# LayerNorm rows of the last two blocks as bf16 rows in DRAM, read back by 32 transposing DMAs

## What is computed

```
proj = h @ w_in                                  # q, k, v, c_gate, b_gate, u
attn = sliding_window_attention(rope(q), rope(k), v, sinks)     # window 128
conv = b_gate * causal_conv3(c_gate * u)
mixed = concat([rms_norm(attn), rms_norm(conv)])
h = layer_norm(ALPHA * h + mixed @ w_out)        # LayerNorm 1
ffn = (silu(h @ w_gate) * (h @ w_up)) @ w_down
h = layer_norm(ALPHA * h + ffn)                  # LayerNorm 2
```

## Time and profile before

| | us |
|---|---|
| median of 3 runs | 2705.77 |
| the profiled execution, by the same measure | 2704.75 |
| its span, slowest core (core 6) | 2703.7 |
| spans of the eight cores | 2693.0 to 2703.7 |
| first half (four blocks), by the first gate/up matmul | 0 to 864.5 |
| feed-forward half | 864.5 to the end |

### The profile page before, as it was taken

The page is one execution under the profiler, slowest core; times in us unless marked ns, Lnnn a source line. Parts: engine busy times, 40 slices in busy tenths (PEclk is TensorE's granted clock), DMA queues, the critical chain, the costliest instruction groups (busy, mean ns, idle before and its releaser), DMA issues.

```text
span 2703.7 us, 33712 instructions; the slowest of 8 cores (2693.0 to 2703.7 us)
## 1 busy us (share of the span) xinstructions
PE 2641.0 (98%) x13266; PEld 1213.2 (45%) x13266; DVE 716.1 (26%) x1454; ACT 497.8 (18%) x922; POOL 99.5 (4%) x191
## 2 busy tenths in 40 slices
PE   6999999998999999999999999999999999999998
PEld 2444444443444444444444444444444444444443
DVE  1445454553553300111111111124200111111026
ACT  1433433432432200000000001122100000000021
POOL 1010010010000000000000000000000000000000
PEclk9999999999999999999999999999999999999999
DMA  9999999999999795334554435557833354434352
GB/s 161 186 187 182 198 184 192 196 184 182 205 189 205 160 250 89 60 66 77 94 86 71 79 59 132 91 106 206 186 64 65 65 102 78 82 67 80 61 106 109
DMA packets 46619, 347.36 MB, mean 128 GB/s; under 512 B 4864, under 2 KB 4992, under 8 KB 19072
## 3 DMA queue, kind: packets, MB, share of 16 engines
q0 software_dynamic: 26928, 256.39, 56.9%
q1 hardware_dynamic: 19536, 88.82, 9.5%
HBM read 559.62 MB, written 41.94 MB: 222 GB/s over the span
## 4 chain that ended last, share of the span: by engine, by line
PE 93%; DMA 4%; DVE 1%; issue 1%; ACT 0%; POOL 0%; DVEq 0%; ACTq 0%; POOLq 0%
PE ps L316 92%; DMA w<-w_qkv 4%; PE ps L320 1%; DVE rowsf L357 0%; DVE atok L342 0%; ACT pT L336 0%; DVE y L357 0%; DVE small L622 0%; DVE ropeA L342 0%; ACT y L336 0%; DVE small L342 0%; DVE zc L342 0%; DVE ropeB L342 0%; POOL xT L366 0%; DVE h1Ts L360 0%
## 5 line engine op out<-in xcount | busy, mean ns | idle before, releaser
L316 PE MATMUL ps<-h1T,w 128*128 128x512 bf16 x5632 | 1216.9, 379 | 0.0
L316 PEld LDWEIGHTS ps<-h1T,w 128*128 128x128 bf16 x5632 | 550.9, 98 | 663.6
L316 PE MATMUL ps<-w,actT 128*128 128x512 bf16 x2640 | 571.6, 379 | 0.0
L316 PEld LDWEIGHTS ps<-w,actT 128*128 128x128 bf16 x2640 | 258.3, 98 | 311.5
L342 DVE TENSOR_TENSOR actT<-ps,sg 128x512 bf16<-128x512 f32 x176 | 121.8, 692 | 1026.4 <-PE ps L316 1009.2
L336 ACT ACTIVATE sg<-ps 128x512 f32<-128x512 f32 x176 | 105.1, 597 | 1320.4 <-PE ps L316 1315.2
L316 PE MATMUL ps<-xT,w 128*128 128x512 bf16 x1536 | 344.9, 380 | 0.0
L316 PEld LDWEIGHTS ps<-xT,w 128*128 128x128 bf16 x1536 | 147.6, 98 | 181.1 <-issue 14.0
L316 PE MATMUL ps<-w,mT 128*128 128x512 bf16 x1024 | 222.3, 379 | 0.0
L357 DVE SCALAR_TENSOR_TENSOR rowsf<-rowsf,ps 128x512 f32<-128x512 f32 x128 | 88.0, 688 | 468.1 <-PE ps L316 468.1
L316 PE MATMUL ps<-w,xT 128*128 128x512 bf16 x768 | 177.4, 388 | 31.8 <-DMA w<-w_qkv 29.3
(11 more groups left out here) (102 smaller groups left out, 858.1 us busy)
## 6 DMA issues: line engine op xcount, KB each, us to landing
w<-w_gu POOLq DMA_DIRECT2D x44, 2048.0 KB, 16.0
w<-w_cbu POOLq DMA_DIRECT2D x32, 1536.0 KB, 32.8
w<-w_down POOLq DMA_DIRECT2D x30, 1408.0 KB, 12.0
w<-w_out POOLq DMA_DIRECT2D x32, 1024.0 KB, 24.6
w<-w_qkv POOLq DMA_DIRECT2D x18, 1024.0 KB, 43.8
h_scr<-rows SPq DMA_DIRECT2D x16, 1024.0 KB, 22.0
rowsf<-h_scr SPq DMA_DIRECT2D x16, 1024.0 KB, 24.2
xT<-xT_c POOLq DMA_DIRECT2D x16, 512.0 KB, 36.7
```

Source lines behind the costliest of these rows:

```text
L316: pr.add("pe", lambda e: e.matmul(out.ap, lhsT=lhsT.ap, rhs=rhs.ap, start=start, stop=stop), r=[lhsT, rhs], w=[out])
```

## The change

For blocks 2 and 3 `tr` is no longer called. `cast` writes the bf16 copies of the four tiles into four different buffers, `h1b[0]`, `h1b[1]`, `stg[0]`, `stg[1]`, and stores each as 128 rows of 4 KB to a new DRAM tensor `h1b_scr`. `h1T_load(1)` reads that tensor with 32 transposing DMAs on SP's queue, each from 512 rows of 256 bytes to 128x512 bf16, in the place of two plain loads of 2 MB. Blocks 0 and 1, and `h1T_load(0)`, are as they were.

```diff
+    h1b_d = nc.dram_tensor("h1b_scr", [1024, D], BF16, kind="Internal")
-    h1T_d = nc.dram_tensor("h1T_scr", [4, 128, 8192], BF16, kind="Internal")
+    h1T_d = nc.dram_tensor("h1T_scr", [2, 128, 8192], BF16, kind="Internal")
...
+    stg = [Region(addr[id(xpA)][0] + 4096 * i, total).sb(f"stg{i}", 2048, BF16) for i in range(2)]
...
     def ln1_tail(p, t, banks):
-        hb = h1b[t % 2]
+        hb = h1b[t % 2] if p < 2 or t < 2 else stg[t - 2]
         def cast():
             store(h1_d[(4 * p + t) * 128:(4 * p + t + 1) * 128, :], full(rows[t], 2048), ("h1", t), w=[("dh1", 4 * p + t)])
             acopy(full(hb, 2048), full(rows[t], 2048))
+            if p >= 2:
+                r0 = (4 * (p - 2) + t) * 128
+                store(h1b_d[r0:r0 + 128, :], full(hb, 2048), ("h1b", t), w=[("dh1b", 4 * (p - 2) + t)])
...
     def h1T_load(b_):
         for th in range(2):
+            if b_ == 1:
+                for c in range(16):
+                    out = V(h1T, th * 8192 + c * 512, [[1, 512]])
+                    src = DAP(h1b_d, th * 512 * D + c * 128, [[D, 512], [1, 128]])
+                    pr.add("sp", lambda e, out=out, src=src: e.dma_start_transpose(out=out.ap, in_=src), r=[("dh1b", 4 * th + i) for i in range(4)], w=[out], dma=("h1Tt", th, c))
+                continue
             load("sp", V(h1T, th * 8192, [[1, 8192]]), h1T_d[2 * b_ + th, :, :], ...)
...
             bg.setdefault(2 * t + 2, []).append(cast)
-            bg.setdefault(2 * t + 4, []).append(tr)
+            if p < 2:
+                bg.setdefault(2 * t + 4, []).append(tr)
```

## The result

Five runs of the changed kernel have a median of 2727.94 us, five of the kernel before on the same chip 2704.44 us. The ratio is **1.0086, 95% interval 1.0073 to 1.0099**: 0.9% slower, within the 2% that count as the same, but with an interval that lies clear of 1. The forecast was 2732 us. (A ratio leaves out runs that were disturbed; a median quoted beside one holds them, and can lie higher.)

What follows compares the result with a forecast made beforehand. TensorE, busy 98% of the span, bounds the kernel, with landings of `rows` stores at the path's edge. 2704.75 + 27.5 + 2.7 - 3.6 = 2731.4 us profiled, 2732 as median; range 2697 to 2752.

Steps and rivals of the forecast that it cites:

- The stall: Start of block 3: bf16 stores on SP's queue delay the landings of `rows`, so `ob` comes 27.5 us later.
- The rival by bytes: Block 3, SP's queue: a half-size store takes 6.5 us and `rows3` lands 19.4 us late; no chance given.
- the first step: Block 3, first `pT`: one bf16 store of 11.7 us ahead moves the landing of `rows1` from 703.3 to 715.0.
- The size of the shift: Block 3, `ob`, which started at 729.42: 27.5 us later than before, between 19.4 and 35.1.
- the relief: Block 3, before `rows3` lands: POOL's last load lands at 754.5, then SP's queue has the engines to itself.
- The clock behind the last stop: Block 3, after TensorE's last stop: low clock adds 2.7 us, between 0 and 8.
- What is removed: Eight transpose groups: four in the feed-forward half save 0.89 us each, 3.6 in all; four in block 3 give nothing.
- The transposing DMAs: 32 DMAs before pass 1: hidden within 165.5 us; bounds 26, 83 and 282 us, landing in 1 to 5 us each.
- No stall: Block 3: small stores slip through, landings of `rows` do not move, only removals count, about 2698 us; chance 0.15.
- Late transposing DMAs: First gate/up group of pass 1: TensorE waits for them, slower by over 2%, 2848 at the upper price; chance 0.13.
- A second stall at `usb` or `zc`: Block 3: their waits, or loads of `xpA` and `xpB` behind the stores, stall again, about 2750 us; chance 0.04.

Runs made afterwards that it cites:

- the 32 KB stores: Kernel before plus one 32 KB store to an unused tensor behind each store of `rows` of block 2: 2712.85 us, ratio 1.0073.
- the doubled small stores: Kernel before plus two 32 KB stores, not one, behind each store of `rows` of block 2: 2707.36 us, ratio 1.0059.
- the last two runs: Changed kernel with `rows` stores on two queues, late bf16 stores from free buffers, short final wait list: 0.9981; kernel before with two queues and short list: 1.0007.
- the four free buffers: Changed kernel with bf16 copies in `xpA` and upper `mT`, so `usb` and `zc` wait for no bf16 store; store order unchanged: 2716.2 us, ratio 1.0089.

## Why the prediction was right

The sum added 27.5 + 2.7 - 3.6 = 26.6 us to the kernel before, and 23.5 were measured (2727.94 - 2704.44). The mechanism was right. That the number came so close is in part luck: the sum was made for core 6, and there the span grew by only 2719.0 - 2703.7 = 15.3 us, 11 less than forecast. The time of the run stayed near the forecast because another core became the slowest. Step by step:

**The stall: mechanism right, its last part too long.** Forecast from core 6 of the kernel before, and what the changed kernel's core 5 shows, where the first store lands at 688.3 in the place of 690.3: `rows1` 715.0, landed 713.3; the second bf16 store 726.7, landed 724.9; `rows2` 739.7, landed 737.7; the third bf16 store 751.4, landed 749.0; `rows3` 756.5 to 757, landed 752.9. The price of a bf16 store, 11.7 us, was 11.9, 11.6 and 11.3. The rival by bytes asked for 6.5; the 32 KB stores settle it, with 11.7 us for a sixteenth of the bytes. On the other cores the first step holds and the last does not. From `rows0` to `rows1` 24.7 us were forecast and are 24.2 to 25.0 on all eight; from `rows1` to `rows2` 24.7, and are 19 to 24; from `rows2` to `rows3` about 17, and are 5 to 15. On core 6 the third bf16 store took 2.8 us in the place of 11.7.

**The size of the shift, by core: too large.** I had worked it out on core 6, and there `ob` moved only 16.7 us, from 729.42 to 746.07. On core 5 it moved 31.3 (721.7 to 753.0), on core 2 36.4, on the eight in the mean 23.3. But part of this came before the stores: the first store of `rows` is issued 6.6 us later on core 5 than in the trace of before (672.52 for 665.96), 10.9 later on core 2 and 2.8 earlier on core 6, although up to there the two kernels run the same instructions. Counted from that issue to `ob`, the stall adds 24.8 us on core 5, 25.6 on core 2, 19.4 on core 6 and 18.5 in the mean, with 27.5 forecast; no core reaches it. Two things had been left out. Cores do not stand at the same place in a given execution: before, core 6 had been the latest at `ob` by 3 to 13 us. And the relief comes more than once. I had it only behind POOL's last load, near the end; in fact POOL's packets already thin out in the second stop. The queues from 725 to 735, core 5 and then core 6:

```profile
q0 software_dynamic: 86, 0.88, 55.2%
q1 hardware_dynamic: 288, 1.60, 46.2%
```

```profile
q1 hardware_dynamic: 451, 2.05, 75.0%
q0 software_dynamic: 48, 0.45, 26.2%
```

From 680 to 700 the two were even, in the earlier trace rows and on core 5 now (252 and 247). Here SP has 288 to 86 and 451 to 48, and the core with more relief lost less. It is the mechanism that the doubled small stores showed in full. What the run lost is neither core's shift but the distance between the slowest of before, core 6, and the slowest of after, core 5: 2727.0 - 2703.7 = 23.3 us.

**The clock behind the last stop: mis-sized.** I had added 2.7 us. The row of 32 matmuls behind the second stop took 8.47 us against 7.08 for the next 32 of the same form, but that loss lies under the next landing, as argued. Behind the last stop, of 4.90 us, 16 matmuls took 3.89 against 3.62: 0.3 us; the mean granted clock was 0.76 from 756.4 to 763 and 1.00 from 763 to 775. The first gate/up matmul moved by 30.3 us on core 5, a microsecond less than `ob`: before, TensorE had waited 1.64 us right ahead of it there, and now it does not. I had forecast 25 to 30; over the eight cores it is 15 to 37, the differences of start included.

**What is removed: right.** From the first gate/up matmul to the down groups it is 1648.91 - 889.17 = 759.74 us now and was 1627.85 - 864.54 = 763.31: 3.57 us less, for four groups of 0.89. The four groups in block 3 gave nothing under the stall, as said. With the stall gone part of them comes through: 2.3 us from the first store of `rows` to `ob`, between the last two runs.

**The transposing DMAs: hidden, right.** 51.9 us in a row against bounds of 26, 83 and 282, and a landing of 4.4 us in the median against 1 to 5. The estimate of 168 us from the Trainium skill's 1309 ns for each 128x128 (VectorE: DVE Perf Modes, The three transpose paths) is not what a row of 32 costs here: 128 such pieces in 51.9 us are 0.41 us a piece, and the measurement decides. The experiment that issued them 37 us ahead shows that the cover, and not their price, made them free.

**Not foreseen: the tail.** 36 semaphores more stand in the list that SP waits for at the end. From the end of the last issue to the end of the span it is now 2727.0 - 2721.08 = 5.9 us, and was 2703.7 - 2700.02 = 3.7, alike on all eight cores. Runs with 78, 82 and 94 semaphores in the list have tails of 3.9, 4.1 and 5.1 us. The timelines of SP's last stores, of after and of before (start, length of the whole row of issues):

```profile
2661.19 59.89 SPq L371 DMA_DIRECT2D out_c<-rowsf  x14
```

```profile
2661.70 38.32 SPq L369 DMA_DIRECT2D out_c<-rowsf  x9
```

So the sum on core 5 is +30.3 - 3.57 + 2.2 = +28.9 us, and its span went from 2698.1 to 2727.0. Of the 30.3 us, 6.6 are the later start. The tail's 2.2 us and the 2.4 us too many for the clock offset each other. The larger error, the stall itself, was hidden by the start of the slowest core: in the mean of the eight cores the span grew by 21.1 us, from 2698.7 to 2719.8, and 4.8 of these lie ahead of the first store of `rows`.

**The rivals.** No stall: dead, by the stops above. Late transposing DMAs: not here, but real as soon as their cover shrinks to 37 us, where they cost 1.1% of the run beyond the stall (1.0196 against 1.0086). A second stall at `usb` or `zc`: dead, by the four free buffers. `xpA` was issued at 754.24 and nothing waited for it.

A fixed price for each DMA was not among the rivals; the loads of 2 KB rows in the trace of before speak against it.

Open: why cores 2 and 5 had less relief than the others, and why the cores reach the first store of `rows` at other times in the two executions.

## What to carry to other kernels

A queue that is backed up beside heavy loads gives out turns, not bytes: before adding a small store to it, count its packets (here 144 for any store of 128 rows), and look at what waits for the landing of the large ones behind it, above all where their source bytes are shared in time. Free buffers don't help against that; another queue, or a place behind the store that somebody waits for, does. And size a stall on every core, because the slowest core after the change need not be the slowest before, and a forecast for one core can be right for the run by luck.

## What the runs showed of the hardware that I had not expected

- A store of 128 rows of 256 bytes (32 KB) took 11.7, 11.1 and 8.5 us of a backed-up queue, nearly as long as one of 512 KB (11.9, 11.6, 11.3). Both have 144 packets. A load of 1 MB in rows of 2 KB took 26.0 us there, with 521 packets.
- Two such stores in the place of one cost no more (1.0059 against 1.0073): the earlier stop let POOL's queue run dry, with 2 packets against 1091 in 12 us.
- Three queues shared evenly: 305, 310 and 300 packets in 30 us.
- Transposing DMAs do not take turns one for one. From 1650 to 1655, beside a load of `w_down`, SP's queue shows 559 packets to POOL's 73, and even so they are slowed: 559 packets are about one DMA, while alone 1235 passed in 3 us. The load of `w_down` landed in 10.7 us (11.9 before). The mean was 1.6 us for each DMA there, and 2.2 beside loads of gate/up weights.
- A long list of semaphores at the end costs time: 2.2 us for 36 more (74 to 110), 0.06 us each. It is not the same for each: 86 fewer saved 3.6 us, and 50 fewer (74 to 24) saved 1.1 to 1.4. That the first part of the list passes while the last store still lands would explain it, and is not shown.
